# Half-precision scatter products interleaved with a weight unit's fp32 products, alternating high and low products, and six sparse rows moved to a later stage

## The chip, the core and the metric

The kernel runs on one core of one Trainium2 chip. The metric is the device time of one execution in microseconds. Before the change it is 1623.44 us, the median of 3 runs (1622.75 to 1623.86).

## The reference

The reference is a small model on one sequence of 256 tokens with 1024 features, everything in fp32. Cut to what matters here:

```
x = mixer(x); x = swiglu_ffn(x)              # layer 0: sparse attention beside a state-space mixer
x = short_conv(x); x = swiglu_ffn(x)         # layer 1
x = rms_norm(x, final_norm)
x = x + merged(hgrn2(h), dilated(h)) @ w_out # layer 2
h2 = rms_norm(x, norm2_g)
q = h2 @ w_q; s = q . sub_keys               # 8 heads, 2 x 128 keys
idx, gate = top 16 of the sums of two top 16 # 128 of the 16384 experts per token
a = gelu(u[idx] . h2) * gate
x = x + sum(a * v[idx])
```

u and v have 16384 rows of 1024 features each, 64 MB each, and are the larger part of what is read.

## The kernel before

**Weights.** All dense weights come as 529 units of 128 x 1024 fp32 (512 KB) in one stream, through a ring of 4 slots that SyncE fills. A unit is worked on in two halves of 512 columns. For each half ScalarE rounds it to a high part (`w_hi`, L1559), then GpSimd (L700), or VectorE in the last stage (L2905), subtracts to get a low part (`w_lo`). There are 4 half slots of either. TensorE computes high weights by high input, high weights by low input, and low weights by high input, and sums the three in a PSUM bank; this stands in for a full fp32 product. Each matmul is a weight load (PEld in the profile) and a product (PE).

**Helpers on TensorE.** `feature` (L793, L798) makes 256-column products. `feature_apart` (L835, L840) puts the high and low inputs side by side: 4 products of 2n columns with high weights in a half, then 4 of n columns with low weights. `rows_product` (L793, L798 too, 512 columns) has the input as stationary operand and the weights moving: for both token halves two products with high weights, then for both one with low weights. `feature_tokens` is `feature` on the first T = 224 tokens.

**The experts.** The tables u and v are taken densely for 224 tokens and by gathered rows for the last 32 tokens ("picks"). There are 128 chunks of 128 experts.
- The early stage: 72 units of u (`feature_apart`, n = 224) while VectorE finds the top experts. ScalarE's `follow` rounds the halves two units ahead.
- The build stage: 56 groups and 56 units of u. A group `scatter(j)` is 8 fp16 products of 128 columns (L1478) that put the gates of four tokens into bank `G{j % 3}`; the unit behind it is `feature_tokens`, 24 products of 224 columns (16 in L793, 8 in L798). VectorE makes the one-hot operands (L2862, L2865), and takes 20 picks of u rows (`pick`, L2845) against a copy in PSUM. GpSimd fetches the rows with indirect DMAs.
- The late stage: 128 units of v (`late_unit`), a half being 4 products of 448 columns (L1499) and then 4 of 224 (L1505), one pair for each of 8 banks. VectorE splits the halves, takes the other 12 picks of u rows in the units up to 30, and from unit 37 on the 32 picks of v rows.

The order of everything is written out by hand. `PICK_GROUPS`, `PICK_UNITS` and `FETCH_UNITS` say at which group or unit a pick or a fetch is.

**Layer 2.** `l2_token` is ten units by `rows_product` and `token`, `l2_mix` 24 units by `feature` into banks mix0 to mix3. ScalarE computes norms, copies and exponentials between its roundings.

Of the kernel before, what the change touches and what calls it, by code (L numbers as in the profile page):

```python
# [25 lines left out]
U32 = mybir.dt.uint32  # L26
# [45 lines left out]
PICK_GROUPS = [7 + 5 * s // 2 for s in range(20)]  # L72
PICK_UNITS = [2 + (13 * s) // 5 for s in range(PICKED - 20)] + [37 + (8 * s) // 3 for s in range(PICKED)]
FETCH_UNITS = {PICK_GROUPS[s - FETCH] + 3: s for s in range(FETCH, 20 + FETCH) if PICK_GROUPS[s - FETCH] + 3 < GATED}
# [83 lines left out]
def bank_turns():  # L158
# [49 lines left out]
    out += [(f"mix{p}", 4 + p, 3) for p in range(4)] + [(f"gates{p}", 4 + p, 4) for p in range(2)]  # L208
# [40 lines left out]
def build(nc, stream, x, vec, row, row2, kv_w, br_w, key_w, u_rows, v_rows, gain_row, spill, out):  # L249
# [8 lines left out]
    with ctx:  # L258
# [506 lines left out]
        def _(pe):  # L765
# [61 lines left out]
            def feature_apart(dst, phase, e, i=0, after=None, n=S):  # L827

                for half in range(2):
                    pe.wait_ge(*half_rounded(phase, e, i, half))  # L830
                    for c in range(4):
                        k = 4 * half + c
                        if after is not None and k % 2 == 0:
                            pe.wait_ge(*read_out(f"hT{after}_{k // 2}"))
                        mm(dst[:, 0:2 * n], high_weights(phase, e, half, slice(c * P, (c + 1) * P)), h[:, k, :, 0:n],  # L835
                           start=k == 0, stop=False, skip_group_check=True)
                    pe.wait_ge(*half_split(phase, e, i, half))
                    for c in range(4):
                        k = 4 * half + c
                        last = mm(dst[:, 0:n], low_weights(phase, e, half, slice(c * P, (c + 1) * P)), h_hi[:, k, 0:n],  # L840
                                  start=False, stop=k == KC - 1, skip_group_check=True)
                    last.then_inc(halves_used, 1)

            def feature_tokens(dst, phase, e, i, n):

                for half in range(2):
                    pe.wait_ge(*half_rounded(phase, e, i, half))
                    for c in range(4):
                        k = 4 * half + c
                        by_high(dst[:, 0:n], high_weights(phase, e, half, slice(c * P, (c + 1) * P)),  # L850
                                (h_hi[:, k, 0:n], h_lo[:, k, 0:n]), k == 0)
# [31 lines left out]
            def rows_product(n, phase, e, lhs, first, final, i=0, after=None, opens=False, between=None):  # L883

                for h in range(2):
# [5 lines left out]
                    for t in range(NT):  # L891
                        if opens:
# [541 lines left out]
            def experts():  # L1434
# [24 lines left out]
                for phase, at in (("peer_early0", 0), ("peer_early1", PHASES["peer_early0"].iters)):  # L1459
                    with pe.Fori(0, PHASES[phase].iters) as i:  # L1460
                        for q in range(4):
                            pe.wait_ge(*before_turn(f"early{q}", i + at))
                            feature_apart(bank(f"early{q}"), phase, q, i, n=T)
# [6 lines left out]
                def scatter(g, i):  # L1470

                    j = i * BUILD_GROUPS + g
                    name = f"G{j % 3}"
                    pe.wait_ge(*before_turn(name, j // 3))
                    pe.wait_ge(ev("one_hot"), j + 1)
                    for n in range(4):
                        for part in (1, 0):
                            last = mm(bank(name)[:, n * P:(n + 1) * P], OH1_parts[:, j % 2, n, :, part],  # L1478
                                      OH2[:, j % 2, n, :], start=part == 1, stop=part == 0)
                    last.then_inc(*fills(name))  # L1480

                for i in range(BUILD_ITERS):
                    for g in range(BUILD_GROUPS):
                        scatter(g, i)
# [63 lines left out]
        def _(act):  # L1548
# [55 lines left out]
            def norm_late(n, gain, name=None):  # L1604
# [3 lines left out]
                for t in range(NT):  # L1608
                    square(t)
                    if name:  # L1610
                        follow(f"{name}_head", 0, 0, (t,))
# [1457 lines left out]
```

## Time and profile before

| | |
|---|---|
| median of 3 runs | 1623.44 us |
| the profiled execution | 1623.38 us |
| its span | 1621.6 us |
| TensorE busy | 1603.8 us, 99% |
| weight loads busy | 1470.8 us, 91% |
| GpSimd busy | 1117.8 us, 69% |
| VectorE busy | 1009.1 us, 62% |
| ScalarE busy | 962.2 us, 59% |
| granted TensorE clock | 1.000 (2.4 GHz) |

The busy time of TensorE is a union of overlapping products, and each product's record includes its way through the array. So a short gap between two products does not show as idle time; the step from one product to the next has to be read from their starts or ends.

### The profile page before, as it was taken

The numbers are of one execution on the slowest core, as the hardware profiler recorded it, in microseconds if no ns is written. First come the engines' busy times: TensorE is split into PE (matmuls) and PEld (weight loads), VectorE is DVE, ScalarE is ACT, GpSimd is POOL, SyncE is SP. The second block draws the span as 40 slices with busy tenths as digits, with TensorE's granted clock in tenths as the row PEclk, the third lists the DMA queues.
The fourth block names the chain that finished last, engine by engine and source line by source line (L and its number), as shares of the span: only waits on it lengthen the run. The fifth ranks groups of instructions, "written<-read, shape, count | busy, mean of one in ns | idle before, by whom it ended". The sixth has DMA issues, their size and how long they took to land.

```text
span 1621.6 us, 31369 instructions
## 1 busy us (share of the span) xinstructions
PE 1603.8 (99%) x10758; PEld 1470.8 (91%) x10758; DVE 1009.1 (62%) x2240; ACT 962.2 (59%) x1917; POOL 1117.8 (69%) x895
## 2 busy tenths in 40 slices
PE   8999999999999999999999999999999999999999
PEld 8898888889988888799998999989999999999998
DVE  2985432334343323756443398988888788889997
ACT  5664755555465555666653777776555566666664
POOL 8455899998989999887654699999999711112110
PEclk9999999999999999999999999999999999999999
DMA  6233455555545555454352466657888888888995
GB/s 237 96 130 118 156 195 184 191 188 166 188 163 191 192 184 193 157 186 140 130 196 80 142 214 216 205 197 235 262 274 265 276 285 290 271 306 301 332 333 176
DMA packets 104257, 333.98 MB, mean 206 GB/s; under 512 B 12144, under 2 KB 26672, under 8 KB 103888
## 3 DMA queue, kind: packets, MB, share of 16 engines
q1 hardware_dynamic: 94304, 294.53, 53.6%
q0 software_dynamic: 9696, 37.91, 7.4%
q8 instruction: 65, 1.06, 0.3%
q14 instruction: 48, 0.39, 0.1%
q10 hardware_dynamic: 144, 0.08, 0.0%
HBM read 324.38 MB, written 7.47 MB: 205 GB/s over the span
## 4 chain that ended last, share of the span: by engine, by line
PE 83%; POOL 5%; issue 5%; DVE 4%; ACT 2%; DMA 0%; POOLq 0%; SPq 0%; DVEq 0%; ACTq 0%
PE bank L793 21%; PE bank L835 11%; PE bank L798 10%; PE bank L1499 10%; PE bank L840 6%; POOL w_lo L700 5%; PE bank L1505 5%; PE banks_and L793 4%; PE banks_and L1499 3%; PE banks_and L798 2%; PE banks_and L1505 2%; PE bank L1478 2%; PE bank L772 1%; PE banks_and L1389 1%; ACT w_hi L1559 1%
## 5 line engine op out<-in xcount | busy, mean ns | idle before, releaser
L700 POOL TENSOR_TENSOR w_lo<-ring,w_hi 128x512 fp32r<-128x512 f32 x802 | 1037.2, 1309 | 216.3 <-ACT w_hi L1559 182.6
L1559 ACT ACTIVATE w_hi<-ring 128x512 fp32r<-128x512 f32 x1058 | 660.7, 630 | 498.5 <-PE bank L798 263.2
L835 PE MATMUL bank<-h_high_and_low,w_hi 128*128 128x512 f32 (+1 forms) x1280 | 335.2, 383 | 0.3 <-ACT w_hi L1559 0.3
L793 PE MATMUL bank<-h_high_and_low,w_hi 128*128 128x256 f32 (+1 forms) x2192 | 308.2, 283 | 0.6 <-ACT arena L1868 0.6
L793 PEld LDWEIGHTS bank<-h_high_and_low,w_hi 128*128 128x128 f32 x2192 | 276.4, 192 | 3.7 <-issue 1.8
L835 PEld LDWEIGHTS bank<-h_high_and_low,w_hi 128*128 128x128 f32 x1280 | 220.8, 189 | 25.5 <-DVE h_high_and_low L2127 1.4
L840 PEld LDWEIGHTS bank<-h_high_and_low,w_lo 128*128 128x128 f32 x1280 | 192.6, 189 | 22.0 <-POOL w_lo L700 2.0
L840 PE MATMUL bank<-h_high_and_low,w_lo 128*128 128x256 f32 (+1 forms) x1280 | 198.6, 277 | 0.5 <-POOL w_lo L700 0.5
L1499 PE MATMUL bank<-A_high_and_low,w_hi 128*128 128x448 f32 x768 | 198.6, 367 | 0.0
L2905 DVE TENSOR_TENSOR w_lo<-ring,w_hi 128x512 fp32r<-128x512 f32 x256 | 176.1, 689 | 30.2 <-ACT w_hi L1559 20.3
L798 PE MATMUL bank<-h_high_and_low,w_lo 128*128 128x256 f32 (+1 forms) x1096 | 172.8, 280 | 0.3 <-POOL w_lo L700 0.3
L712 POOL DMA_INDIRECT arena<-v_rows,rows x32 | 39.6, 1237 | 184.8 <-DVE arena L2852 152.6
L798 PEld LDWEIGHTS bank<-h_high_and_low,w_lo 128*128 128x128 f32 x1096 | 148.4, 192 | 0.5 <-POOL w_lo L700 0.5
L1499 PEld LDWEIGHTS bank<-A_high_and_low,w_hi 128*128 128x128 f32 x768 | 135.1, 189 | 9.4
L1505 PE MATMUL bank<-A_high_and_low,w_lo 128*128 128x224 f32 x768 | 125.9, 272 | 0.0
L1505 PEld LDWEIGHTS bank<-A_high_and_low,w_lo 128*128 128x128 f32 x768 | 115.4, 190 | 4.1
L2524 DVE TENSOR_TENSOR bank<-bank,arena 128x256 f32<-128x256 f32 x44 | 19.0, 433 | 146.0 <-ACT arena L1834 145.8
L2862 DVE TENSOR_SCALAR XN<-bank,selT 128x128 f32<-128x128 f32 x224 | 76.5, 405 | 23.7 <-PE bank L1478 23.7
L2076 ACT ACTIVATE A_high_and_low<-arena 128x224 fp32r<-128x224 f32 x127 | 49.7, 391 | 63.5 <-PE bank L1505 62.3
L793 PE MATMUL bank<-w_hi,h_high_and_low 128*128 128x512 f32 (+1 forms) x304 | 77.2, 376 | 0.1
L1499 PE MATMUL banks_and<-A_high_and_low,w_hi 128*128 128x448 f32 x256 | 75.2, 375 | 0.0
L712 POOL DMA_INDIRECT arena<-u_rows,rows x32 | 32.3, 1010 | 54.3 <-DVE arena L2845 50.2
(454 smaller groups left out, 2193.1 us busy)
## 6 DMA issues: line engine op xcount, KB each, us to landing
ring<-stream SPq DMA_DIRECT2D x529, 512.0 KB
spill<-mask_parts SPq DMA_DIRECT2D x56, 112.0 KB
XN<-spill SPq DMA_DIRECT2D x56, 112.0 KB, 6.0
arena<-branch_w POOLq DMA_DIRECT2D x1, 3072.0 KB, 12.4
X<-x SPq DMA_DIRECT2D x2, 512.0 KB, 4.0
arena<-kv_w SPq DMA_DIRECT2D x1, 1024.0 KB, 7.0
out<-X SPq DMA_DIRECT2D x4, 256.0 KB, 2.1
arena<-row POOLq DMA_DIRECT2D x1, 512.0 KB, 6.4
```

The lines of the kernel that those rows point to most:

```text
L700: nc.gpsimd.tensor_tensor(w_lo[:, hs, :], ring[:, slot(phase, e), k * HALF:(k + 1) * HALF], w_hi[:, hs, :].bitcast(F32), ALU.subtract) \
L712: nc.gpsimd.indirect_dma_start(fetched[:, s % FETCH, :], None, (u_rows if s < PICKED else v_rows), bass.IndirectOffsetOnAxis(pick_index[:, ...
L793: mm(dst, a, b, start=start and n == 0, stop=False, skip_group_check=True)
L798: return mm(dst, a, b, start=False, stop=stop, skip_group_check=True)
L835: mm(dst[:, 0:2 * n], high_weights(phase, e, half, slice(c * P, (c + 1) * P)), h[:, k, :, 0:n], start=k == 0, stop=False, skip_group_check ...
L840: last = mm(dst[:, 0:n], low_weights(phase, e, half, slice(c * P, (c + 1) * P)), h_hi[:, k, 0:n], start=False, stop=k == KC - 1, skip_grou ...
L1499: mm(bank(f"acc6_{k}")[:, 0:2 * T], high_weights(phase, at % 4, half, slice(c * P, (c + 1) * P)), A2[:, :, n % 2, 0:T], start=n == 0, stop ...
L1505: last = mm(bank(f"acc6_{k}")[:, 0:T], low_weights(phase, at % 4, half, slice(c * P, (c + 1) * P)), A_hi[:, n % 2, 0:T], start=False, stop ...
L1559: A(w_hi[:, half_slot(phase, e, k), :], ring[:, slot(phase, e), k * HALF:(k + 1) * HALF], ACT.Copy).then_inc(rounded, 1)
L2076: A(A_hi[:, nxt % 2, 0:T], chunk(GATED + nxt if nxt < EARLY else nxt - EARLY), ACT.Copy).then_inc(ev("late_high"), 1)
L2862: V.tensor_scalar(OH1[:, n % 2, k, :], iota, selT[:, 0, tok:tok + 1], selT[:, 2, tok:tok + 1], ALU.is_equal, ALU.mult)
L2905: V.tensor_tensor(w_lo[:, hs, :], ring[:, slot(phase, e), k * HALF:(k + 1) * HALF], w_hi[:, hs, :].bitcast(F32), ALU.subtract) \
```

## The change

- `scatter` is cut into 8 steps, and `feature_tokens` calls one after each of the 8 high-weight products of its first half. Before, the 8 fp16 products stood ahead of the unit.
- `feature_apart` gets a lag: in the early stage (lag 1) the half's order is high, high, low, high, low, high, low, low. In the other stages (lag 3) it is as before.
- `late_unit` alternates high and low products, and waits for the low weights ahead of the half.
- `rows_product` does all three products of one token half, then the three of the other; the wait for the low weights comes after two products in place of four.
- 14 in place of 20 picks are in the build, 18 in place of 12 in the late stage ahead of the v rows, which begin at unit 39 in place of 37.
- On ScalarE some roundings are placed between other work (norms, `l2_token`, `l2_mix`, `peer_q`), the four decay exponentials stand at unit 13, and in the early stage the conversion of the keys and an exponential are at units 59 and 62 in place of 58. mix0 to mix2 lie in banks 6, 4, 5 in place of 4, 5, 6.

```diff
-PICK_GROUPS = [7 + 5 * s // 2 for s in range(20)]
-PICK_UNITS = [2 + (13 * s) // 5 for s in range(PICKED - 20)] + [37 + (8 * s) // 3 for s in range(PICKED)]
+IN_BUILD = 14
+PICK_GROUPS = [7 + 7 * s // 2 for s in range(IN_BUILD)]
+PICK_UNITS = [2 + 2 * s for s in range(PICKED - IN_BUILD)] + [39 + (8 * s) // 3 for s in range(PICKED)]
...
-    out += [(f"mix{p}", 4 + p, 3) for p in range(4)] + [(f"gates{p}", 4 + p, 4) for p in range(2)]
+    out += [(f"mix{p}", (6, 4, 5, 7)[p], 3) for p in range(4)] + [(f"gates{p}", 4 + p, 4) for p in range(2)]
...
+            def high_then_low(lag):
+
+                for step in range(4 + lag):
+                    if step < 4:
+                        yield step, True
+                    if step >= lag:
+                        yield step - lag, False
...
+            def feature_tokens(dst, phase, e, i, n, between):
 
                 for half in range(2):
                     pe.wait_ge(*half_rounded(phase, e, i, half))
                     for c in range(4):
                         k = 4 * half + c
...
+                        for part, x in enumerate((h_hi, h_lo)):
+                            mm(dst[:, 0:n], high_weights(phase, e, half, slice(c * P, (c + 1) * P)), x[:, k, 0:n],
+                               start=k == part == 0, stop=False, skip_group_check=True)
+                            if half == 0:
+                                between(2 * c + part)
...
                         by_high(bank(f"{n}_{2 * t + h}")[:], high_weights(phase, e, h, slice(0, HALF)),
-                                (lhs[0][:, cols], lhs[1][:, cols]), first, swap=True)
-                    pe.wait_ge(*half_split(phase, e, i, h))
-                    for t in range(NT):
-                        cols = slice(t * P, (t + 1) * P)
+                                (lhs[1][:, cols], lhs[0][:, cols]), first, swap=True)
+                        if t == 0:
+                            pe.wait_ge(*half_split(phase, e, i, h))
                         last = by_low(bank(f"{n}_{2 * t + h}")[:], low_weights(phase, e, h, slice(0, HALF)),
...
+                def scatter(j, step):
+
+                    name, n, part = f"G{j % 3}", step // 2, 1 - step % 2
+                    if step == 0:
+                        pe.wait_ge(*before_turn(name, j // 3))
+                        pe.wait_ge(ev("one_hot"), j + 1)
+                    last = mm(bank(name)[:, n * P:(n + 1) * P], OH1_parts[:, j % 2, n, :, part],
+                              OH2[:, j % 2, n, :], start=part == 1, stop=part == 0, skip_group_check=True)
...
                     for half in range(2):
-                        pe.wait_ge(*half_rounded(phase, at % 4, at // 4, half))
+                        pe.wait_ge(*half_split(phase, at % 4, at // 4, half))
...
-                        pe.wait_ge(*half_split(phase, at % 4, at // 4, half))
-                        for c in range(4):
-                            k = 4 * half + c
                             last = mm(bank(f"acc6_{k}")[:, 0:T],
...
-                    for t, after in enumerate((24, 58)):
+                    for t, after in enumerate((24, 59)):
...
-                    for t, after in enumerate((32, 58)):
+                    for t, after in enumerate((32, 62)):
...
-                    if n == PICK_UNITS[PICKED - 21] + 1:
+                    if n == PICK_UNITS[PICKED - IN_BUILD - 1] + 1:
```

## Rows read from the trace of the kernel before

**Rows 1.** The page: busy time, share of the span, instructions of TensorE.

```profile
PE 1603.8 (99%) x10758; PEld 1470.8 (91%) x10758; DVE 1009.1 (62%) x2240; ACT 962.2 (59%) x1917; POOL 1117.8 (69%) x895
```

**Rows 2.** Waits of TensorE, the longest group: us in total, times, longest.

```profile
PE bank L772 <- DMA X<-x: 5.8, 1, 5.8
```

**Rows 3.** Windows of the end of the early, the build, the late stage.

```profile
core 0: us, PE busy (x) PEld busy (x) DVE busy (x) ACT busy (x) POOL busy (x), PEclk, DMA share, GB/s
...
1000.00:1100.00 100.00, 98.17 (x613) 90.30 (x611) 88.69 (x268) 72.91 (x163) 98.35 (x78) 1.00 0.62 203
...
1130.00:1284.00 154.00, 154.00 (x1548) 152.67 (x1547) 133.04 (x332) 84.37 (x193) 142.46 (x117) 1.00 0.82 269
1284.00:1607.00 323.00, 323.00 (x2069) 306.59 (x2067) 277.13 (x495) 197.51 (x388) 54.87 (x50) 1.00 0.87 296
```

**Rows 4.** Timeline of TensorE, one group and unit of the build: start, us.

```profile
1130.35 0.62 PE L1478 MATMUL bank<-XN 128*128 128x128 f16 x8
1130.78 1.13 PE L793 MATMUL bank<-h_high_and_low,w_hi 128*128 128x224 f32 x8
1131.75 0.61 PE L798 MATMUL bank<-h_high_and_low,w_lo 128*128 128x224 f32 x4
...
1133.55 0.62 PE L1478 MATMUL bank<-XN 128*128 128x128 f16 x8
```

**Rows 5.** Timeline of narrow windows of the build: single products at both borders.

```profile
1152.59 0.28 PE L798 MATMUL bank<-h_high_and_low,w_lo 128*128 128x224 f32 x1
...
1152.71 0.23 PE L1478 MATMUL bank<-XN 128*128 128x128 f16 x1
...
1153.11 0.22 PE L1478 MATMUL bank<-XN 128*128 128x128 f16 x1
...
1153.14 0.35 PE L793 MATMUL bank<-h_high_and_low,w_hi 128*128 128x224 f32 x1
```

**Rows 6.** The same for weight loads, with a product inside a run.

```profile
1152.70 0.10 PEld L1478 LDWEIGHTS bank<-XN 128*128 128x128 f16 x1
...
1153.11 0.19 PEld L793 LDWEIGHTS bank<-h_high_and_low,w_hi 128*128 128x128 f32 x1
...
1154.10 0.27 PE L798 MATMUL bank<-h_high_and_low,w_lo 128*128 128x224 f32 x1
...
1154.00 0.30 PEld L798 LDWEIGHTS bank<-h_high_and_low,w_lo 128*128 128x128 f32 x2
```

**Rows 7.** Timeline of TensorE, half a unit of the late stage.

```profile
1351.91 0.99 PE L1499 MATMUL bank<-A_high_and_low,w_hi 128*128 128x448 f32 x4
1352.74 0.60 PE L1505 MATMUL bank<-A_high_and_low,w_lo 128*128 128x224 f32 x4
1353.17 0.59 PE L1499 MATMUL banks_and<-A_high_and_low,w_hi 128*128 128x448 f32 x2
...
1351.91 0.38 PE L1499 MATMUL bank<-A_high_and_low,w_hi 128*128 128x448 f32 x1
```

**Rows 8.** Timelines of splits and their users, and the picks by form.

```profile
252.98 0.39 PE L798 MATMUL banks_and<-w_lo,A_high_and_low 128*128 128x512 f32 x1
...
248.76 1.29 POOL L700 TENSOR_TENSOR w_lo<-ring,w_hi 128x512 fp32r<-128x512 f32 x1
...
1350.21 1.29 DVE L2905 TENSOR_TENSOR w_lo<-ring,w_hi 128x512 fp32r<-128x512 f32 x2
...
L2845 DVE SCALAR_TENSOR_TENSOR arena<-arena 128x1024 f32<-128x1024 f32 x11 | 13.4, 1219 | 0.0
```

**Rows 9.** Timeline of TensorE at the first unit of layer 2's mix.

```profile
691.17 1.21 PE L793 MATMUL bank<-h_high_and_low,w_hi 128*128 128x256 f32 x8 [0.56 <-ACT arena L1868]
```

**Rows 10.** Timelines of the early stage's end: ScalarE, VectorE, TensorE.

```profile
1077.21 0.42 ACT L2015 ACTIVATE arena<-arena 128x256 f32<-128x256 uint32 x1 [1.56 <-DVE arena L2788]
...
1080.76 0.40 DVE L2743 TENSOR_TENSOR bank<-bank,arena 128x224 f32<-128x224 f32 x1 [2.28 <-ACT arena L2009]
...
1081.27 0.70 PE L840 MATMUL bank<-h_high_and_low,w_lo 128*128 128x224 f32 x4 [0.28 <-POOL w_lo L700]
...
1100.38 0.87 PE L772 MATMUL banks_and<-ident,arena 128*128 128x128 f32 x6 [1.46 <-DVE arena L2812]
```

More of the change, by code:

```diff
@@ L825, in feature, with feature_apart @@
                         between()
-            def feature_apart(dst, phase, e, i=0, after=None, n=S):
+            def high_then_low(lag):
[4 more added lines that the diff above has]
+                        yield step - lag, False
+            def feature_apart(dst, phase, e, i=0, after=None, n=S, lag=3):
+                for half in range(2):
+                    pe.wait_ge(*half_rounded(phase, e, i, half))
+                    for c, is_high in high_then_low(lag):
+                        k, cols = 4 * half + c, slice(c * P, (c + 1) * P)
+                        if is_high:
+                            if after is not None and k % 2 == 0:
+                                pe.wait_ge(*read_out(f"hT{after}_{k // 2}"))
+                            mm(dst[:, 0:2 * n], high_weights(phase, e, half, cols), h[:, k, :, 0:n],
+                               start=k == 0, stop=False, skip_group_check=True)
+                        else:
+                            if c == 0:
+                                pe.wait_ge(*half_split(phase, e, i, half))
+                            last = mm(dst[:, 0:n], low_weights(phase, e, half, cols), h_hi[:, k, 0:n],
+                                      start=False, stop=k == KC - 1, skip_group_check=True)
+                    last.then_inc(halves_used, 1)
+            def feature_tokens(dst, phase, e, i, n, between):
                 for half in range(2):
@@ L1462, in experts @@
                             pe.wait_ge(*before_turn(f"early{q}", i + at))
-                            feature_apart(bank(f"early{q}"), phase, q, i, n=T)
+                            feature_apart(bank(f"early{q}"), phase, q, i, n=T, lag=1)
                     if at == 0:
@@ L1468, in experts @@
                             transposes(f"sel{t}", [SEL[:, t, w, :] for w in range(3)])
[L1470 to L1480, printed above, removed]
+                def scatter(j, step):
[5 more added lines that the diff above has]
+                              OH2[:, j % 2, n, :], start=part == 1, stop=part == 0, skip_group_check=True)
+                    if step == 7:
+                        last.then_inc(*fills(name))
                 for i in range(BUILD_ITERS):
                     for g in range(BUILD_GROUPS):
-                        scatter(g, i)
                         c = i * BUILD_UNITS + g
                         pe.wait_ge(*before_turn(f"build{c % 2}", c // 2))
-                        feature_tokens(bank(f"build{c % 2}"), "peer_build", g, i, T)
+                        feature_tokens(bank(f"build{c % 2}"), "peer_build", g, i, T, lambda step: scatter(c, step))
                 def late_unit(n):
@@ L1590, in norm_final @@
                     A(XN[:, t, :], X[:, t, :], ACT.Square, accum_out=gstat[:, t:t + 1]).then_inc(ev("final_ssq"), 1)
-                follow("l2_token", 0)
+                    follow("l2_token", 0, 0, (t,))
                 for t in range(NT):
+                    follow("l2_token", 1, 0, (t,))
                     act.wait_ge(ev("x_final"), t + 1)
@@ L1595, in norm_final @@
                     A(XN[:, t, :], X[:, t, :], ACT.Square, accum_out=gstat[:, 2 + t:3 + t]).then_inc(ev("final_ssq"), 1)
-                    follow("l2_token", 1, 0, (t,))
                 for k in range(2):
@@ L1865, in mixer2 @@
                         follow("l2_token", KC)
+                follow("l2_token", KC + 1)
                 act.wait_ge(*unit_used("l2_token", KC + 1))
@@ L1869, in mixer2 @@
                       scale=stat[:, 6 + t:7 + t]).then_inc(*frees(f"tok{4 + t}"))
-                follow("l2_token", KC + 1)
                 act.wait_ge(ev("lb_diff"), 1)
```

76 lines of the change are left out of this document (32 added, 44 removed).

## The prediction

> **What bounds the kernel now.** I read the page first: TensorE is busy 99% of the span, the next engine 69% [rows 1]. Then its waits: the longest group is the load of x at the start, 5.8 us, once [rows 2]. So there is little idle time to win, and the time goes with how fast one product follows another. Then the windows by stage: in the build and in the late stage TensorE is busy every microsecond, at the full clock, with VectorE at 133.0 of 154 us and 277.1 of 323 us and GpSimd at 142.5 of 154 us in the build [rows 3]. Only at the end of the early stage does a second engine stand beside it: GpSimd is busy 98.35 of 100 us there, TensorE 98.17 [rows 3]. Last the timeline, for the steps between products: this is where the change acts.
>
> **The scatter products between the unit's.** One group and unit take 3.20 us (1130.35 to 1133.55). The 8 fp16 products take 0.43 us of it until the unit starts. The first 8 fp32 products take 0.97 us. The other 16 of the unit take 1.80 us (1131.75 to 1133.55), 0.1125 us each; 8 of those would be 0.90 us, so the first 8 are 0.07 us dearer [rows 4]. Single products show why, read by their ends. The last fp32 product ahead of the group ends at 1152.87, the first fp16 one at 1152.94: 0.07 us. The eighth fp16 one ends at 1153.33: 0.39 us for seven, 0.056 each. The first fp32 one ends at 1153.49: 0.16 us [rows 5]. A pair "fp32, fp16" with a border on both sides is thus 0.07 + 0.16 = 0.23 us. In runs of one kind the two are 0.1125 + 0.056 = 0.17 us. One way there and back costs 0.06 us.
>
> The loads say what the 0.06 us is. Within an fp32 run, the next load starts 0.01 us after the product before it starts: a product starts at 1154.10, and the second of the two loads, which last 0.19 us each and end at 1154.30, starts at 1154.11 [rows 6]. So a load lies under the product before it. The fp32 load after the group starts at 1153.11, with the last fp16 product [rows 5, 6], but that product lasts only 0.056 us and the fp32 loads follow at 0.11 us: half of the load sticks out. The first fp16 load starts at 1152.70, 0.11 us after the fp32 product of 1152.59 and not 0.01 us: it does not lie under the fp32 product at all [rows 5, 6].
>
> Before, each unit has one way there and back (in the 3.20 us already). After, it has 8: seven more, 7 x 0.06 = 0.42 us, and 56 units make 23.5 us. No product is saved. Both ends: if the late start of the first fp16 load belongs to its place and not to its kind (it carries the wait for the one-hots), it hides under the fp32 product. The fp32 product behind the group ends at 1153.49; less the 0.28 us that such a record lasts, it began in effect at 1153.21, 0.10 us after the fp16 one of 1153.11 [rows 5]. With 0.11 us for the fp32 product itself a pair is 0.21: 0.04 us more than in runs, 7 x 0.04 x 56 = 15.7 us. If neither load sticks out, a pair is 0.17 and the one border of today goes too: 56 x 0.06 = 3.4 us won. I take 23.5, since each half of it is read from a product of this very kind next to one of the other.
>
> The Trainium skill, "TensorE: Matmul & The Clock Gate", section "Step-by-step: what each phase is for", says that the next tile's weights load while this tile's product runs; in the section "LDWEIGHTS (loading the stationary operand)" a load is given as its columns by 1.2 GHz. By that rule a pair would be the 224-column product at 2.4 GHz, 93 ns, and the 128-column fp32 load, 107 ns: an estimate of 0.20 us and of 12 us for the build. The trace has the fp32 loads at 0.11 us and agrees, but has the fp16 load outside the fp32 product, which the page's rule does not give.
>
> What this could collide with: the group's bank is full about 1.4 us later in its unit. VectorE makes the one-hots of the group after next then (the operands are double), with a whole unit more before their use, and ScalarE copies the gates later; both have shares under 0.87 before and lose 6 picks or gain time from the longer unit. I take 0.
>
> **The picks.** Six picks of 1.22 us (13.4 us for 11, [rows 8]) leave the build and come into the first 37 late units, 93 us. VectorE is 277.1 of 323 us busy in the late stage [rows 3], so 93 us have some 13 free, of which the 7.3 are taken. Cover is VectorE's idle time and the 4 half slots. DMA's share is 0.87 there and 0.82 in the build [rows 3]; six fetches of 128 rows of 4 KB are 3 MB in 93 us, 34 GB/s beside 296, a share of 0.97 at the same rate at worst. Price 0 if both hold; if VectorE were late each time, at most 6 x 1.22 = 7 us. I take 0.
>
> **Late units alternate.** A half is 0.83 us for four high and 0.43 us for four low products, 1.26 together, 0.315 a pair [rows 7]. The first high one ends after 0.38 us and the fourth after 0.99, so the steps between them are 0.203 and the four are 0.02 us longer than four such steps: the first load sticks out of the short low product before it, as do those of three of the lows (0.11 us, the pace of loads). Alternating, the loads of all lows lie under high products, and those of all highs under lows: again four exposed in a half. So the sum is the same; a load exposed costs from 0 to 0.01 us more than a low's. Ends: 0.01 us a half either way, 256 halves, 2.6 us up or down. I take 0. The wait for the low weights moves up by 0.83 us. The split of the half starting at 1351.91 ended at 1350.90, the first of two of 0.69 us begun at 1350.21 [rows 7, 8]: 1.0 us ahead even though a pick of 1.22 us ended just before. Nothing is charged; without that cover it would be the missing time once for each pick.
>
> **Early units.** With lag 1 the first low product comes after two highs, not four: 2 x 0.21 = 0.41 us sooner. Here GpSimd's splits are the second bound [rows 3, 10]: at 1081.27 TensorE waited for one. A later TensorE finds the next split ready by as much, so the 0.41 us is paid once and not in each unit. I take +0.4 us, between 0 and 1.
>
> **rows_product.** The same products. The low weights are wanted after two products, 0.46 us sooner. In the feed-forward units the split of the half whose low product starts at 252.98 ended at 250.05 [rows 8], 2.9 us ahead, so 0 for the 52 down units. In `l2_token` the splits are late and the rounding order changes too; up to 0.5 us either way, taken as 0.
>
> **Layer 2's order and the keys.** mix0 no longer lies in the bank that ScalarE's L1868 must empty: TensorE's 0.56 us of idle time there, with the gap's hidden part 0.7 us, go [rows 9]. At the early stage's end ScalarE waits 1.56 us for VectorE with its queue of roundings behind it, VectorE then 2.28 us for ScalarE, and TensorE at last 1.46 us for VectorE's indices [rows 10]. With the conversion one unit later the first wait goes, and VectorE's chain moves up. What is late next is the exponential, now at unit 62. I take 1.5 us won, between 0 and 2.9. Other moved roundings: 0.
>
> **The sum**, against the profiled execution: 1623.4 + 23.5 + 0.4 - 0.7 - 1.5 = 1645.1 us. That execution (1623.38, span 1621.6) lies 0.06 us from the median, so it holds for the median.
>
> **Rivals.**
> 1. The fp16 load hides under the fp32 product when it carries no wait. The build costs 15.7 us: 1623.4 + 15.7 - 1.8 = 1637. For it: only the first fp16 load, the one with the wait, was seen behind an fp32 product. Against: an fp32 load with a wait of its own (each half's first) does not start late.
> 2. The other side: the loads run further ahead. If TensorE takes an fp32 load two products early while an fp16 one goes by, pairs cost 0.17 and the border of today goes: 1623.4 - 3.4 - 1.8 = 1618, faster. It decides if the pair is under 0.17 us. The same page's section "Back-to-back issue gap" speaks of a 64-deep window through which loads and products are pipelined. Against it stand rows 5 and 6: during the eight fp16 products there was time to load ahead, and the fp32 load still started with the last of them. For it: no row shows true alternation.
> 3. The late stage runs out of VectorE or DMA with six more picks and an earlier wait: 1645.1 + 7 = 1652.
>
> **How the numbers follow.** That the border costs in full gets 0.63, rival 1 0.18, rival 2 0.12, rival 3 0.07. The range reaches over the first two: below 1637 with 5 us for the late units and the small terms, 1632; above 1645 with 1 us of rounding in the border, 2.6 for the late units and 2 for gains that do not come, 1651. It leaves out rivals 2 and 3. A measurement of this kernel tells 0.2%, 3.2 us. Rival 2 gives faster by 0.3%, nearly all of its 0.12; same gets 0.03; slower the rest, 0.85.
>
> **What the profile after would show.** If right: units of the build at 3.6 us, fp16 loads starting 0.11 us behind fp32 products, pairs at 0.23; late units at 2.52; no wait of L1868 at the mix; less wait for L2812. Wrong, if a build unit stays at or under 3.2, or late units lengthen with waits on L2905.

## Result and the profile after

The changed kernel takes 1646.22 us, the median of 4 runs (1644.4 to 1647.26), beside 1623.2 us for the kernel before on the same chip: a ratio of 1.0142, 95% interval [1.0129, 1.0154]. It is slower by 23.0 us, where 21.7 were forecast. The profiled execution is that of 1647.26 us, with a span of 1645.5 us. Of all the executions in this text two were slow throughout and are in no median: one of the kernel before (6154.18 us) and one of the kernel with the block in the middle of the unit (2493.86 us).

The page of the changed kernel, its first part. TensorE has the same 10758 products, and 23.4 us more busy time than in [rows 1]; the others are about where they were.

```profile
span 1645.5 us, 31369 instructions
PE 1627.2 (99%) x10758; PEld 1484.4 (90%) x10758; DVE 1011.6 (61%) x2240; ACT 965.0 (59%) x1915; POOL 1117.5 (68%) x895
```

Its timeline of TensorE, one unit of the build with its eight scatter products (L1489) between high-weight products (L862):

```profile
1203.24 0.23 PE L1489 MATMUL bank<-XN 128*128 128x128 f16 x1
1203.29 0.35 PE L862 MATMUL bank<-h_high_and_low,w_hi 128*128 128x224 f32 x1
1203.48 0.23 PE L1489 MATMUL bank<-XN 128*128 128x128 f16 x1
1203.52 0.35 PE L862 MATMUL bank<-h_high_and_low,w_hi 128*128 128x224 f32 x1
1203.71 0.23 PE L1489 MATMUL bank<-XN 128*128 128x128 f16 x1
...
1206.88 0.23 PE L1489 MATMUL bank<-XN 128*128 128x128 f16 x1
```

The first scatter products of two units are 3.64 us apart (1203.24, 1206.88), where a group and unit took 3.20 in [rows 4]. Within the unit a pair is 0.23 us (1203.24, 1203.48, 1203.71). And this is so in every pair: in all 56 units the seven steps are 0.230 to 0.235 us, though only the group's first product carries a wait.

The weight loads of the same stretch answer to [rows 6]:

```profile
1203.13 0.28 PE L862 MATMUL bank<-h_high_and_low,w_hi 128*128 128x224 f32 x1
1203.24 0.10 PEld L1489 LDWEIGHTS bank<-XN 128*128 128x128 f16 x1
...
1203.25 0.20 PEld L862 LDWEIGHTS bank<-h_high_and_low,w_hi 128*128 128x128 f32 x1
...
1203.47 0.10 PEld L1489 LDWEIGHTS bank<-XN 128*128 128x128 f16 x1
1203.48 0.23 PE L1489 MATMUL bank<-XN 128*128 128x128 f16 x1
```

The fp16 load begins 0.11 us behind the start of the first fp32 product (1203.24 after 1203.13). The next record starts early and is longer, 0.35 us; taken as its end less 0.28, as in the prediction, that product began at 1203.36, and the load of 1203.47 is again 0.11 us behind it. No fp16 load comes at 0.01, as an fp32 load in a run does. It does not lie under the product before it.

The same halves of the weight stream in both traces say where the time went. After minus before, read at the last product of a half: +0.1 us when layer 2 begins, +0.55 at the end of `l2_token`, -0.27 behind the mix's first wait (the one of [rows 9]) and about so up to the early stage, +0.19 at its 57th unit, -1.40 at its 67th, +0.95 at its end, +25.96 at the end of the build (1289.90 before), +26.5 behind the late stage's first half unit, +24.0 at the last product's end (1617.93 before). So the pieces are: layer 2 -0.4, the early stage +1.2, the build +25.0, the passage to the late stage +0.5, the late stage -2.5.

Two of the changed kernel's waits of TensorE, in the whole execution (the first is at the early stage's end, the second in `l2_token`), then its timeline at the transposes of the indices, and the windows around them:

```profile
PE banks_and L774 <- DVE arena L2824: 2.3, 1, 2.3
...
PE banks_and L800 <- POOL w_lo L702: 0.9, 2, 0.7
```

```profile
1099.76 1.13 PE L774 MATMUL banks_and<-ident,arena 128*128 128x128 f32 x6 [2.26 <-DVE arena L2824]
```

```profile
1097.00:1100.00 3.00, 0.74 (x6) 0.54 (x6) 2.93 (x4) 1.23 (x3) 3.00 (x4) 1.00 0.61 193
1100.00:1104.00 4.00, 4.00 (x18) 3.77 (x17) 3.83 (x11) 1.81 (x5) 1.25 (x2) 0.57 0.32 120
1104.00:1112.00 8.00, 8.00 (x52) 7.59 (x52) 5.30 (x10) 5.27 (x12) 7.77 (x6) 1.00 0.60 183
```

The wait of 1.46 us for VectorE in [rows 10] is now 2.26 us, and behind it the granted clock is 0.57 for 4 us. The two levels are 2.4 and 1.2 GHz, so some 3.4 of the 4 us went at the lower (0.43 x 2 x 4), which costs up to 1.7 us. Before, no stretch fell to it.

In the late stage the pairs alternate, at 0.21 and 0.10 us; four of them are 1.253 us, where [rows 7] had 1.26:

```profile
1376.05 0.37 PE L1510 MATMUL bank<-A_high_and_low,w_hi 128*128 128x448 f32 x1
1376.26 0.26 PE L1513 MATMUL bank<-A_high_and_low,w_lo 128*128 128x224 f32 x1
1376.36 0.38 PE L1510 MATMUL bank<-A_high_and_low,w_hi 128*128 128x448 f32 x1
```

### The profile page after: what moved, and what is told of

Its sections match the earlier page's. It is cut to its first block, busy times and chain, and to the rows that moved or that the text cites. A ratio compares the mean times of both kernels' runs of the same rounds, so it can differ in the third digit from the quotient of the medians.

```text
span 1645.5 us, 31369 instructions
## 1 busy us (share of the span) xinstructions
PE 1627.2 (99%) x10758; PEld 1484.4 (90%) x10758; DVE 1011.6 (61%) x2240; ACT 965.0 (59%) x1915; POOL 1117.5 (68%) x895
## 4 chain that ended last, share of the span: by engine, by line
PE 93%; DVE 3%; ACT 2%; issue 1%; POOL 1%; DMA 0%; SPq 0%; DVEq 0%; ACTq 0%
PE bank L846 17%; PE bank L795 14%; PE bank L800 10%; PE bank L1510 10%; PE bank L851 9%; PE bank L862 7%; PE bank L1513 5%; PE banks_and L795 5%; PE banks_and L1510 3%; PE banks_and L800 2%; PE bank L1489 2%; PE banks_and L1513 2%; PE bank L774 1%; PE banks_and L1402 1%; ACT w_hi L1567 1%
## 5 line engine op out<-in xcount | busy, mean ns | idle before, releaser
L846 PE MATMUL bank<-h_high_and_low,w_hi 128*128 128x512 f32 (+1 forms) x1280 | 368.4, 385 | 0.0
L1510 PE MATMUL bank<-A_high_and_low,w_hi 128*128 128x448 f32 x768 | 248.6, 375 | 0.0
L851 PE MATMUL bank<-h_high_and_low,w_lo 128*128 128x256 f32 (+1 forms) x1280 | 244.2, 276 | 0.0
L846 PEld LDWEIGHTS bank<-h_high_and_low,w_hi 128*128 128x128 f32 x1280 | 221.4, 190 | 23.1 <-DVE h_high_and_low L2139 1.4
L851 PEld LDWEIGHTS bank<-h_high_and_low,w_lo 128*128 128x128 f32 x1280 | 217.5, 189 | 26.5 <-POOL w_lo L702 2.9
L1513 PE MATMUL bank<-A_high_and_low,w_lo 128*128 128x224 f32 x768 | 202.0, 263 | 0.0
L795 PE MATMUL bank<-h_high_and_low,w_hi 128*128 128x256 f32 x1296 | 185.6, 286 | 0.0
L800 PE MATMUL bank<-h_high_and_low,w_lo 128*128 128x256 f32 (+1 forms) x1096 | 176.7, 283 | 0.3 <-POOL w_lo L702 0.3
L795 PEld LDWEIGHTS bank<-h_high_and_low,w_hi 128*128 128x128 f32 x1296 | 167.4, 191 | 3.0 <-issue 1.5
L862 PE MATMUL bank<-h_high_and_low,w_hi 128*128 128x224 f32 x896 | 165.4, 307 | 0.0
L800 PEld LDWEIGHTS bank<-h_high_and_low,w_lo 128*128 128x128 f32 x1096 | 149.0, 192 | 0.5 <-POOL w_lo L702 0.5
L1513 PEld LDWEIGHTS bank<-A_high_and_low,w_lo 128*128 128x128 f32 x768 | 146.3, 191 | 0.0
L862 PEld LDWEIGHTS bank<-h_high_and_low,w_hi 128*128 128x128 f32 x896 | 144.6, 196 | 0.0
L1489 PE MATMUL bank<-XN 128*128 128x128 f16 x448 | 103.5, 231 | 0.0
```

What stands on the lines that cost most here:

```text
L795: mm(dst, a, b, start=start and n == 0, stop=False, skip_group_check=True)
L800: return mm(dst, a, b, start=False, stop=stop, skip_group_check=True)
L846: mm(dst[:, 0:2 * n], high_weights(phase, e, half, cols), h[:, k, :, 0:n], start=k == 0, stop=False, skip_group_check=True)
L851: last = mm(dst[:, 0:n], low_weights(phase, e, half, cols), h_hi[:, k, 0:n], start=False, stop=k == KC - 1, skip_group_check=True)
L862: mm(dst[:, 0:n], high_weights(phase, e, half, slice(c * P, (c + 1) * P)), x[:, k, 0:n], start=k == part == 0, stop=False, skip_group_chec ...
L1510: mm(bank(f"acc6_{k}")[:, 0:2 * T], high_weights(phase, at % 4, half, slice(c * P, (c + 1) * P)), A2[:, :, n % 2, 0:T], start=n == 0, stop ...
```

## Experiments

Each was timed against the kernel before on the same chip (medians 1622.0 to 1622.1 us, 1622.9 for the last). "Span" comparisons below are inside one trace, since the start of an execution alone varies by 1 to 2 us.

**The interleave alone.** The kernel before with the new `feature_tokens` and `scatter`, and nothing else.

```diff
-                        scatter(g, i)
                         c = i * BUILD_UNITS + g
...
-                        feature_tokens(bank(f"build{c % 2}"), "peer_build", g, i, T)
+                        feature_tokens(bank(f"build{c % 2}"), "peer_build", g, i, T, lambda step: scatter(c, step))
```

> The kernel before with one part of the change: the 8 fp16 scatter products between the first half's fp32 ones; all else as before. Border theory (each way from fp32 to fp16 and back costs 0.064 us, seven more a unit, 56 units): 1623.2 + 25 = 1648 us, build unit 3.64 us. Rival (the interleaving is not the cause, or only together with the fewer picks or the moved waits): under 1640 us.

Measured: 1648.46 us, 1.016 [1.0144, 1.0175], 26.4 above the kernel before. From the first scatter product to the first late one it is 204.26 us (1110.08 to 1314.34), before 178.82 (1111.19 to 1290.01). The interleave is the loss, and more than all of it.

**All but the interleave.** The changed kernel with the group ahead of its unit again.

> The changed kernel with the 8 fp16 products back ahead of the unit; everything else of the change stays. Border theory: 1646.2 - 25 = 1621 us, 2 us under the kernel before, of which the late stage's alternation gives 2.3. Rival (other parts of the change cost time too, the late picks for one): above 1624 us.

Measured: 1619.46 us (11 runs, 1618.12 to 1622.11), 0.9983 [0.9974, 0.9992]. The rest of the change wins 2.6 us. Its five runs with a clock of 1.000 took 1618.1 to 1619.0 us, the six others, at 0.998 or 0.999, took 1619.5 to 1622.1.

**Two and two.** The changed kernel with the scatter products in four pairs, one behind every second high-weight product.

```diff
-                        feature_tokens(bank(f"build{c % 2}"), "peer_build", g, i, T, lambda step: scatter(c, step))
+                        feature_tokens(bank(f"build{c % 2}"), "peer_build", g, i, T, lambda step: step % 2 and (scatter(c, step - 1), scatter(c, step)))
```

> The changed kernel, but the scatter products come in pairs: two fp32, two fp16, and so on, 4 ways there and back in a unit in place of 8. Border theory: 4 x 0.064 x 56 = 14.3 us less than the change, 1632 us, build unit 3.38 us. Rival (the cost is that of work between the unit's products, whatever its grouping, or a wait at the first): no linear fall, 1640 us or more, or all of it gone at once, 1622 us.

Measured: 1631.55 us, 1.0051 [1.0035, 1.0066]. Its timeline of TensorE:

```profile
1199.88 0.29 PE L1489 MATMUL bank<-XN 128*128 128x128 f16 x2
1199.98 0.46 PE L862 MATMUL bank<-h_high_and_low,w_hi 128*128 128x224 f32 x2
1200.28 0.29 PE L1489 MATMUL bank<-XN 128*128 128x128 f16 x2
```

Two and two take 0.40 us; with 0.1125 and 0.056 for their steps in runs, 0.337, one border is 0.063. Three borders more than a block in each of 56 units are 10.6 us by that. From the first scatter product to the first late one it is 189.48 us here (1112.00 to 1301.48) and 178.81 in the kernel with all but the interleave (1110.58 to 1289.39): 10.7 more, of which 10.5 lie in the build and the rest at its borders to other stages. The medians are 12.1 apart. The cost goes by the number of borders, not of products.

**One block, in the middle of the unit.** All eight behind the eighth high-weight product.

```diff
-                        feature_tokens(bank(f"build{c % 2}"), "peer_build", g, i, T, lambda step: scatter(c, step))
+                        feature_tokens(bank(f"build{c % 2}"), "peer_build", g, i, T, lambda step: step == 7 and [scatter(c, s) for s in range(8)])
```

> The changed kernel, but all 8 scatter products in one row behind the first half's eighth high product: in the middle of the unit, with one way there and back. Border theory: the place costs nothing, the same as with the block ahead of the unit, 1619.5 us, 27 us under the change. Rival (being inside the unit costs, through the bank that changes in the middle of a sum or through the later gates): 1622 us or more.

Measured: 1621.32 us, 0.9991 [0.9982, 1.0001], nearer to the rival's 1622 than to the 1619.5 of the theory. From the first to the last scatter product the build takes 176.03 us (1112.51 to 1288.54), before 176.04 (1111.19 to 1287.23). So inside the build the place costs nothing, as long as it is one block. The time above the forecast lies outside. Seven of the nine runs had a clock below 1.000. And the passage to the late stage costs 0.5 us, here and in every kernel whose last scatter products stand inside their unit. The last bank of gates is full later in its unit: ScalarE begins to copy it 2.06 us ahead of the first late product (1288.79, 1290.85), just the time that the copy and three steps of VectorE and ScalarE behind it take, where it had 2.45 us with the block ahead of the unit (1286.94, 1289.39). So TensorE waits for the first late activations:

```profile
1290.85 0.47 PE L1510 MATMUL banks_and<-A_high_and_low,w_hi 128*128 128x448 f32 x1 [0.26 <-DVE A_high_and_low L2924]
```

**Scatter products in fp32.** The changed kernel, whose eight products read parts of h in fp32 in place of the one-hots in fp16. The gates are left out of the result by this; products, banks and order are the same.

```diff
-                    last = mm(bank(name)[:, n * P:(n + 1) * P], OH1_parts[:, j % 2, n, :, part],
-                              OH2[:, j % 2, n, :], start=part == 1, stop=part == 0, skip_group_check=True)
+                    last = mm(bank(name)[:, n * P:(n + 1) * P], h_hi[:, n, 0:P],
+                              h_hi[:, n, P:2 * P], start=part == 1, stop=part == 0, skip_group_check=True)
```

> The changed kernel, interleaved as in the change, but each of the 8 scatter products a unit takes fp32 operands of the same 128 x 128 shape (parts of the high input) in place of the fp16 one-hots; the gates are left out of the result by it. Border theory (the price is that of a change of type: an fp16 load does not lie under an fp32 product, and an fp32 load does not fit under a short fp16 one): all loads are hidden and follow at 0.112 us, a pair is 0.224 in place of 0.231, a unit 32 x 0.112 = 3.59 us, 3 us less than the change: 1643 us. Rival (the price is that of changing banks or of a short product between long ones, whatever the type): pairs of 0.28, a unit near 4.0 us, 1668 us.

Measured: 1642.74 us, 1.0125 [1.0109, 1.014]. Its timeline, products and one load:

```profile
1201.30 0.27 PE L862 MATMUL bank<-h_high_and_low,w_hi 128*128 128x224 f32 x1
1201.31 0.19 PEld L1489 LDWEIGHTS bank<-h_high_and_low 128*128 128x128 f32 x1
...
1201.41 0.23 PE L1489 MATMUL bank<-h_high_and_low 128*128 128x128 f32 x1
1201.48 0.32 PE L862 MATMUL bank<-h_high_and_low,w_hi 128*128 128x224 f32 x1
1201.64 0.23 PE L1489 MATMUL bank<-h_high_and_low 128*128 128x128 f32 x1
...
1201.86 0.23 PE L1489 MATMUL bank<-h_high_and_low 128*128 128x128 f32 x1
```

A pair of two fp32 products is 0.225 us, twice the 0.1125 of a run: here no border is left. It is hardly less than the 0.231 with fp16. And the load of the scatter product, in the same place and with the same wait ahead of it, now begins 0.01 us behind the fp32 product (1201.31 after 1201.30), in all 56 x 8 cases 0.02 us or less, where the fp16 load came at 0.11 to 0.12 us: so its late start goes with its operand, and not with its place, its bank or its wait. The operand changed in two ways, in its type and in its layout (the one-hots are read with a stride of 2 elements, the parts of h without), and no run here parts the two; nor does one show why such a load does not start under an fp32 product. The pairs say what the change did: a scatter product costs 0.056 us among its own kind, and between fp32 products it costs what an fp32 product does, 0.11 to 0.12. fp16 had made the group cheap, and the interleave takes that back.

**The late alternation alone**, and **with the mix's banks and order.** The kernel before with the new `late_unit`; then also mix0 in bank 6, and the rounding of `l2_token`'s last unit ahead of the copies.

```diff
-                        pe.wait_ge(*half_rounded(phase, at % 4, at // 4, half))
+                        pe.wait_ge(*half_split(phase, at % 4, at // 4, half))
...
-                        pe.wait_ge(*half_split(phase, at % 4, at // 4, half))
-                        for c in range(4):
-                            k = 4 * half + c
```

> The kernel before with only the late units changed: high and low products in turn, the low weights waited for ahead of the half. Theory: a pair takes 0.313 us in place of 0.316, so 2.4 us less: 1620.8 us. Rival (the fall of the late stage in the changed kernel comes from something else, such as its later start): 1623.2 us, within 0.5.

Measured: 1619.35 us (11 runs), 0.9981 [0.9972, 0.999]: 2.7 us won.

> The kernel before with two parts of the change alone: the late units' alternation, and mix0 to mix2 in banks 6, 4, 5 with the last l2_token rounding ahead of the two copies. Theory: 2.5 us for the first as measured, and 0.7 us for the wait that goes at the first mix unit: 1618.8 us on a chip where the kernel before takes 1622.1. Rival (the wait only moves to the next unit): the same as the alternation alone, 1619.4 us.

Measured: 1618.73 us, 0.998 [0.9971, 0.9989]. In the traces the mix gives 0.8 us (from -0.32 to -1.13 against the kernel before, at the wait of [rows 9]).

**The picks alone**, and **`rows_product` alone**, each in the kernel before.

> The kernel before with the picks alone moved: 14 in the build, 18 in the late units ahead of the rows of v. My step: nothing, since VectorE and DMA have room in both stages: 1622 us, within 1, and no wait of TensorE in the late stage. Rival (rival 3 of the prediction): up to 7 us more.

Measured: 1621.94 us beside 1622.01, 1.0003 [0.9993, 1.0012]. Nothing.

> The kernel before with rows_product alone changed: all three products of a token half, then those of the other, and the wait for the low weights after two products. My step: nothing in the feed-forward units, up to 0.5 us more in l2_token, where the low weights come late: 1622.3 us. Rival (the new order is quicker or slower by itself, product by product, as in the late units): over 1 us either way, spread over the feed-forward stages.

Measured: 1622.19 us, 1.0001 [0.9992, 1.001]. In the trace it loses 0.45 us in `l2_token` (from -1.97 to -1.53 against the kernel before) and nothing elsewhere.

**Keys and exponential back at unit 58**, and **the early units' lag back at 3**, each in the kernel that has all but the interleave.

```diff
-                    for t, after in enumerate((24, 59)):
+                    for t, after in enumerate((24, 58)):
...
-                    for t, after in enumerate((32, 62)):
+                    for t, after in enumerate((32, 58)):
```

> The changed kernel with the scatter block back ahead of the unit and, beside it, the key conversion and the exponential back at early unit 58. Theory (moving them only shifts TensorE's waits from the roundings at 1080 us to the indices at 1098 us, where a gap of 2.3 us lets the clock fall to 1.2 GHz in many runs): no clock below 1.000 in any run, and a median within 1 us of the 1619.5 us with them at 59 and 62, with less spread. Rival (the move wins the 1.5 us that I predicted): 1621 us.

Measured: 1619.84 us (11 runs, all at a clock of 1.000), 0.9985 [0.9976, 0.9995]. TensorE's wait for the transposes is 1.13 us here. The move to 59 and 62 is worth about a microsecond where the clock holds, and is lost where it falls: no difference in the median beyond the noise.

```diff
-                            feature_apart(bank(f"early{q}"), phase, q, i, n=T, lag=1)
+                            feature_apart(bank(f"early{q}"), phase, q, i, n=T)
```

> The changed kernel with the scatter block ahead of the unit and, beside it, the early units' order as before (four high, four low). Theory: the changed kernel loses some 0.4 us against GpSimd in the early stage, so the early stage is 0.4 us shorter here; but TensorE then waits as much longer for the indices, and the total stays at 1619.5 us. Rival (the alternation wins in the early stage as it does in the late): 1 us more, 1620.5 us.

Measured: 1622.31 us, 0.9995 [0.9975, 1.0015], but not one group of times: five runs at 1617.0 to 1619.0 us (clock 1.000) and five at 1625.6 to 1627.3 (0.997 or 0.998). The lag's own price shows in the traces, from layer 2's mix to the early stage's 47th unit: +0.5 us with lag 1 (-1.86 to -1.35), nothing with lag 3 (-1.67 to -1.68). The profiled run is one of the longer five. Its timelines of VectorE, GpSimd and TensorE:

```profile
1088.16 6.58 DVE L2762 TENSOR_TENSOR arena<-arena 128x128 f32<-128x128 f32 x1
```

```profile
1083.29 11.31 POOL L702 TENSOR_TENSOR w_lo<-ring,w_hi 128x512 fp32r<-128x512 f32 x9
```

```profile
1103.28 1.54 PE L774 MATMUL banks_and<-ident,arena 128*128 128x128 f32 x6 [7.62 <-DVE arena L2823]
```

One VectorE operation of 128x128 lasts 6.58 us and ends at 1094.74, 0.14 us after a row of nine splits on GpSimd. VectorE's indices are late by as much, TensorE waits 7.62 us, and the clock is low behind it. I come back to this below.

**The gap filled.** All but the interleave, and the transposes of the indices and gates one early unit later, ScalarE's copies of them with them.

```diff
                         for q in range(4):
+                            if at and q == 1:
+                                for t in range(NT):
+                                    pe.wait_ge(ev("chosen"), NT)
+                                    pe.wait_ge(*before_turn(f"sel{t}"))
+                                    transposes(f"sel{t}", [SEL[:, t, w, :] for w in range(3)])
...
-                    if u == before_last:
+                    if u == before_last + 1:
```

> This is the change without its scatter interleave (median 1619.5), with TensorE's transposes of the chosen indices and gates one early unit later, and ScalarE's copies of them later by the same unit. In that kernel TensorE stood idle for 2.31 us ahead of the transposes at 1098.22, and ran at half its clock from 1098.85 to about 1102.5 after it. My theory: the gap is a wait for VectorE's last choice, a unit of 2.5 us of TensorE's work lies ready that could fill it, and the slow clock follows from the gap. Then both go: 2.3 us for the gap and some 1.2 to 1.8 us for the 3.6 us at half clock, so 1615.5 to 1616.5, with a granted clock of 1.000 in every run. The first one-hot rows were done at 1102.9 and wanted at 1110.58, so that 2.5 us later costs nothing. Rival one: the slow clock has another cause, and only the gap goes: 1617.2, with clocks of 0.998 in many runs. Rival two: the gap only moves, because the units ahead of the build then wait for something else that the gap had hidden (the split of weights on GpSimd, the buffers of the sums), and the time stays at 1619 to 1620.

Measured: 1616.1 us (5 runs, 1615.58 to 1617.49), 0.996 [0.9946, 0.9973], the clock at 1.000 in every run. Its timeline and windows:

```profile
1099.49 0.38 PE L851 MATMUL bank<-h_high_and_low,w_lo 128*128 128x224 f32 x2
1099.70 0.83 PE L774 MATMUL banks_and<-ident,arena 128*128 128x128 f32 x6
1100.29 0.65 PE L846 MATMUL bank<-h_high_and_low,w_hi 128*128 128x448 f32 x2
```

```profile
1096.00:1100.00 4.00, 4.00 (x28) 3.71 (x28) 3.90 (x6) 2.51 (x7) 4.00 (x5) 1.00 0.57 181
1100.00:1104.00 4.00, 4.00 (x28) 3.81 (x27) 3.83 (x8) 3.39 (x10) 4.00 (x4) 1.00 0.30 116
```

The wait is gone, and so is the slow stretch. From the first early product to the first scatter product it is 183.8 us (924.10 to 1107.93) in place of 187.9 (922.65 to 1110.58): 4.1 us less, 2.3 for the gap and 1.8 for the clock. Both rivals fall: the low clock did come from the gap, and the gap did not move elsewhere. This is the fastest version of the study, 6.8 us below the kernel before.

## Why the prediction was right

Forecast 1645.1 us, slower; measured 1646.22. The step that carries it held, and two small terms did not. That the total came within 1.1 us is in part luck: in the traces the border was 1.5 us dearer than forecast, the early stage's end 2.3, the passage to the late stage 0.5 and `rows_product` 0.4, and the late units were 2.5 cheaper.

- **The border.** Forecast 0.06 us for one way there and back, 7 more in each of 56 units, 23.5 us. Measured 3.64 us a unit and 25.0 us for the stage, so 0.447 a unit and 0.064 a border. The reading of the two single products was right in kind; the term was small by the rounding of the rows to 0.01 us, which the range had. Rival 1 (the late fp16 load was due to its wait) is out: fp16 loads without a wait are as late, an fp32 load with the wait is not, and the pair is 0.231, not 0.21. Rival 2 (the loads run ahead, 0.17 a pair) is out by the same rows. The estimate of 0.20 us a pair fell short too. It came from the rule of the Trainium skill, "TensorE: Matmul & The Clock Gate", section "Step-by-step: what each phase is for", that the next tile's weights load under this tile's product. Here that holds for two fp32 products, as the loads of [rows 6] and of the kernel with fp32 pairs show (0.01 us behind), and not for an fp16 load behind an fp32 product (0.11 us behind).
- **Late units alternate.** Taken as 0 between +2.6 and -2.6; the lower end came, -2.7 us alone and -2.5 in the changed kernel. The step that was mis-sized is "again four exposed in a half": a half is 1.253 us and not 1.263. Alternation leaves steps of 0.213 and 0.100, and the short product of 224 columns is followed at 0.100, below the 0.1125 that such products have among their own kind in the build. 0.010 us a half by 256 halves is 2.6 us.
- **The early stage's end.** Forecast -1.5 and "less wait for L2812", measured +0.8 and more wait: the one step that went the other way. The first half of the argument held: the waits about 1080 went, and TensorE was 1.6 us sooner (from +0.19 to -1.40). But what it arrived at sooner was a wait. The text says "what is late next is the exponential, now at unit 62" and then priced it at nothing. The timelines of VectorE and ScalarE after show its price:

```profile
1089.12 0.40 DVE L2755 TENSOR_TENSOR bank<-bank,arena 128x224 f32<-128x224 f32 x1 [1.42 <-ACT arena L2028]
```

```profile
1086.00 1.28 ACT L2039 ACT_TABLE_LOAD   x1
...
1088.65 0.33 ACT L2028 ACTIVATE arena<-bank 128x224 f32<-128x224 f32 x1
1089.00 1.28 ACT L2014 ACT_TABLE_LOAD   x1
```

  ScalarE loads a table for the exponential, 1.28 us, and VectorE waits 1.42 us for the copy of 1088.65, which stands behind that load, the exponential and two roundings; a second load follows. This price was there before as well (tables at 1077.64 and 1080.64, VectorE's wait of 2.28 us in [rows 10]): the change moved the exponential and did not take it out. From 1070 us to the transposes VectorE's waits of over 0.15 us make 2.6 us before and 1.95 us after, and its chain of indices ends only 0.6 us sooner (transposes at 1099.76, before 1100.38). TensorE's gap grew by 0.8 us to 2.26, and with it came the low clock, which no term had: the other 1.6 of the 2.35 us from -1.40 to +0.95. That the gap causes the low clock is shown by the kernel in which it is filled, and by the one with a gap of 1.13 us, at 1.000 in all its runs.
- **Early lag.** +0.4 forecast, +0.5 measured. It is paid in small steps between the 19th and the 45th unit and not after them, so it is bounded, as reasoned; up to the 18th unit the new order even wins 0.1 us.
- **Mix, L1868 and `rows_product`.** -0.7 forecast for the wait of [rows 9]: it is gone, and 0.8 us with it, alone and in the changed kernel (from +0.55 to -0.27). `rows_product` costs 0.45 in `l2_token`, alone and here (from +0.12 to +0.55): TensorE asks for the low weights two products sooner, and waits 0.66 us for GpSimd at 673.34 where its longest such wait before was 0.35. That was the upper end given, "up to 0.5 us either way", taken as 0.
- **The picks.** 0, and 0 measured. Rival 3 is out: nothing in the late stage waits for VectorE, but for the first unit's activations, 0.26 us. The windows of the changed kernel's build and late stage answer to [rows 3]: VectorE has a smaller share in the build than there (0.73 after 0.86) and a larger one in the late stage (0.89 after 0.86), where it takes the six picks more, and TensorE stays busy every microsecond.

```profile
1130.00:1310.00 180.00, 180.00 (x1585) 170.68 (x1584) 131.09 (x328) 89.66 (x197) 139.04 (x113) 1.00 0.68 218
1320.00:1630.00 310.00, 310.00 (x1981) 295.66 (x1980) 277.09 (x496) 190.34 (x372) 55.03 (x47) 1.00 0.90 309
```

The sum with the measured terms: 25.0 for the border, 0.5 at the late stage's start, where the prediction took 0 for the group's bank being full later in its unit, -2.5, +0.8, +0.5, -0.4 and 0.1 up to layer 2 make 24.0 us. The spans differ by 23.9 and the medians by 23.0.

## What to carry to other kernels

Before products of another kind are put between others, count the borders: what the cheaper kind costs is set by its neighbours, and a block of it keeps it cheap. Two single products read by their ends at an existing border gave the price of 392 new ones to within 6%.

An edit that brings the busiest engine sooner to a join is worth only what the other branch is also sooner; price that branch's next wait, and ask whether ready work can stand in the gap. One unit moved ahead of the transposes gave more than all the retimings on ScalarE together.

## What the hardware showed that was not expected

**A gap of 2.3 us cost its own length and most of that again.** In the profiled runs TensorE's clock stayed at 2.4 GHz after idle times of 1.13 and 1.44 to 1.46 us at this place and fell to 1.2 GHz after 2.26 to 2.32 us. Of the five kernels whose profiled run has this gap of 2.3 us, 23 of 32 executions had a clock below 1.000 (six of eleven of the kernel with all but the interleave). Of the six other kernels, with 1.13 to 1.46 us, none of 58 had; of the kernel before, timed beside them, 2 of 83. So the low clock is likely with the longer gap and rare with the shorter one, and what decides in a single execution is not shown. In the wait of 7.62 us the clock fell while TensorE still stood, and was low for longer: 0.50 and then 0.76 over 10 us, in the windows of the kernel with lag 3:

```profile
1100.00:1104.00 4.00, 0.72 (x4) 0.72 (x5) 3.86 (x7) 1.30 (x4) 3.64 (x3) 0.50 0.41 128
1104.00:1114.00 10.00, 10.00 (x51) 9.40 (x50) 6.46 (x17) 5.33 (x13) 5.25 (x5) 0.76 0.35 108
```

**VectorE can lose its turn to GpSimd several times in a row.** The operation that lasted 6.58 us has two inputs in SBUF. The same one took 1.26 us in the changed kernel and 1.20 before, and another of its size and inputs (L2830, at 1103.57 in the kernel with lag 3, as a row of splits ended) 0.28 us. A split on GpSimd is 1.26 us. In all but this one case (two such operations in each of 14 traces, less L2830 of this one) the operation ended 0.15 us after the split that was running when it began. Here it ended 0.15 us after the fifth split behind that one: 0.13 us until the next split started, 5 x 1.26, and 0.15 make 6.58. The Trainium skill, "SBUF — State Buffer", section "SBUF: two separate sides", says that the two engines share a pair of ports as an exclusive lock, held for a whole instruction, and that a VectorE operation with two SBUF inputs needs it against a GpSimd operation that reads SBUF. The times agree with one wait for one split; that VectorE can be passed over by five further splits while GpSimd goes from one to the next, this trace shows and that section does not say. What decides stays open. In the kernel before, GpSimd's row of splits ran on too, and VectorE got in after one. The case of 6.58 us is the one that began shortest ahead of the next split, 0.13 us; the 26 others had 0.6 us or more. That is one case, and no test of it. That the other four long runs of that kernel have the same cause was not looked at in a trace, only that their times and clocks are those of the profiled one. Nor is it that kernel's alone, if the cause is the same: one of the 27 executions of the kernel before on that chip took 1631.17 us, at a clock of 0.998.
